# Probabilities of a neighbourhood-attention stage: five TensorE transposes per unit replaced by a split in place and one DMA transpose

## What is computed

```
s_loc = einsum('bwhd,biwjhd->bhwij', qr, kwin) * ATTN_SCALE + bias     # 8 x 16 keys around the query
s_ctx = einsum('bwhd,bchd->bhwc', qr, kc) * ATTN_SCALE                 # 256 context keys
p = softmax(concatenate([s_loc, s_ctx], axis=-1))
o = p_loc @ vwin + p_ctx @ vc
```

## Time and profile before

| what | value |
|---|---|
| median of 3 runs | 1250.49 us (1248.52 to 1252.25) |
| span of the profiled execution | 1246.6 us |
| median less the span | 3.9 us (start and end, around the span) |
| PE busy | 1226.5 us (98% of the span) |
| DVE, ACT, POOL busy | 979.6, 653.0, 398.3 us |
| the 32 units: first score to last transpose | about 268 to 380 us |

### The profile page before, as it was taken

The page is one execution under the profiler, slowest core; times in us unless marked ns, Lnnn a source line. Parts: engine busy times, 40 slices in busy tenths (PEclk is TensorE's granted clock), DMA queues, the critical chain, the costliest instruction groups (busy, mean ns, idle before and its releaser), DMA issues. The chain is left out here.

```text
span 1246.6 us, 22702 instructions
## 1 busy us (share of the span) xinstructions
PE 1226.5 (98%) x8085; PEld 668.1 (54%) x8085; DVE 979.6 (79%) x1597; ACT 653.0 (52%) x1231; POOL 398.3 (32%) x385
## 2 busy tenths in 40 slices
PE   7999999999999999999999999999999999999998
PEld 1564656556775666664454555554555554444444
DVE  3879998676778999964479888888888885666587
ACT  2642234556779999963145554455555543412425
POOL 0000000114678988850320444445554430000001
PEclk9999999999999999999999999999999999999999
DMA  9728723235210130121300332322223307997963
GB/s 354 282 87 318 260 78 136 68 87 155 67 35 2 35 136 9 29 86 51 118 34 1 102 102 84 92 85 66 87 90 101 101 28 265 336 339 249 351 228 135
DMA packets 111043, 164.35 MB, mean 132 GB/s; under 512 B 8560, under 2 KB 70000, under 8 KB 109552
## 3 DMA queue, kind: packets, MB, share of 16 engines
q1 hardware_dynamic: 110960, 163.24, 38.5%
HBM read 138.57 MB, written 22.55 MB: 129 GB/s over the span
## 5 line engine op out<-in xcount | busy, mean ns | idle before, releaser
L1327 PE MATMUL PS<-arena 128*128 128x512 f16 (+9 forms) x7485 | 1185.2, 319 | 13.1 <-DMA arena<-in_w_mod 5.7
L1327 PEld LDWEIGHTS PS<-arena 128*128 128x128 f16 (+3 forms) x7485 | 617.3, 100 | 555.3 <-issue 33.5
L3133 DVE SCALAR_TENSOR_TENSOR arena<-arena 128x512 f16<-128x512 f32 x128 | 111.6, 878 | 30.6 <-ACT arena L2361 29.8
L2361 ACT ACTIVATE arena<-arena 128x512 f16<-128x512 f32 x120 | 75.4, 631 | 103.2 <-PE PS L1327 103.2
L2491 ACT ACTIVATE arena<-arena 128x512 f16<-128x512 f32 x77 | 48.1, 629 | 124.7 <-DVE arena L3354 74.6
L3017 DVE TENSOR_REDUCE arena<-PS 128x1 f32<-128x512 f32 (+1 forms) x160 | 106.8, 680 | 3.3 <-PE PS L1327 3.3
L1321 POOL TENSOR_TENSOR arena<-arena 128x1 f32<-128x1 f32 x8 | 4.7, 598 | 231.3 <-DVE arena L3521 227.9
L2262 ACT ACTIVATE arena<-PS 128x512 f16<-128x512 f32 x125 | 75.7, 605 | 2.8 <-PE PS L1327 1.8
L1171 POOL TENSOR_TENSOR arena<-arena 128x512 f16<-128x512 f32 x64 | 74.0, 1158 | 8.0 <-ACT arena L2265 5.4
L3190 DVE TENSOR_TENSOR arena<-PS,arena 128x256 f32<-128x256 f32 (+1 forms) x100 | 55.2, 553 | 25.9 <-PE PS L1327 25.6
L3369 DVE SCALAR_TENSOR_TENSOR arena<-arena 128x512 f16<-128x512 f32 x77 | 52.2, 687 | 18.9 <-ACT arena L2491 18.8
(11 more groups left out here) (227 smaller groups left out, 1321.0 us busy)
## 6 DMA issues: line engine op xcount, KB each, us to landing
...
arena<-lay_bias SPq DMA_DIRECT2D x12, 512.0 KB, 3.9
...
```

What stands on the lines that cost most here:

```text
L1327: return pe.matmul(out, lhsT, rhs, start=start, stop=stop, skip_group_check=True)
L2361: act.activation(block_split(p, b)[:, 0], weight_block(p, b, first), ACT.Copy, scale=WS).then_inc(blk_hi, 1)
L3133: dve.scalar_tensor_tensor(dst[:, 1], src, WS, dst[:, 0], ALU.mult, ALU.subtract).then_inc(blk_lo, 1)
```

## The change

The fp32 probabilities are no longer turned by PE. ACT and DVE take the high and the low fp16 half of the unturned probabilities from SBUF (one instruction each of 640 columns, into `Phl`, three buffers), and SP issues one DMA transpose per unit that turns the 1280 fp16 columns of both halves at once from `Phl` into `PT` (three buffers). It waits for the low half, for the transpose two units earlier and for the weighing three units earlier. `weigh` moves from two slots behind to three, and behind the quarter projection of its slot; `scaled` moves from two behind to four. `scores(k)` waits for `exponentials(k-2)` and no longer for the first piece of `low_p(k-2)`. The bias pieces are issued one at a time between the transposes, the output weights in parts of 256 KB (the first MB between the transposes, the others after the last unit), and four of GpSimd's eight `scale_out` move into the groups 1 to 4 of the next stage. Several buffers move in SBUF, and `exponentials(0)` waits for what lay in the place of `Pb`.

```diff
-        self.banks = [range(0, 3), range(3, 5)]
+        self.third = v % 3
         self.scores_at = 1024 * self.par
-    def turned(self, bank):
-        return 2 * self.v + bank + 1
-    def turned_at(self, bank):
-        if bank == 1:
-            return 512 * (6 + self.par) + 256
-        return self.scores_at + 5 * P
+    def turned_in(self):
+        return 16 * (self.v // 2 + 1 + self.par)
...
-        rcp = f32(2.4375, 2)
+        rcp = f32(2.4375, 8)
...
-        Pb = [f32(o, 5, P) for o in (103, 105.5)]
-        PT = [[f16(o, 5, P) for o in parts] for parts in ((28, 29.25), (30.5, 100))]
-        nearV = [f16(o, 4, HN, 2, HD) for o in (20, 24, 32, Z + 91)]
-        bias = [f32(o, 1024) for o in (4, 8, 36, 40, 44)]
+        Pb = [f32(o, 5 * P) for o in (12, 14.5)]
+        Phl = [f16(o, 2, 5 * P) for o in (100, 102.5, 105)]
+        PT = [f16(o, 2 * 5, P) for o in (46, 48.5, 17)]
+        nearV = [f16(o, 4, HN, 2, HD) for o in (20, 24, 28, Z + 91)]
+        bias = [f32(o, 1024) for o in (4, 8, 32, 36, 40)]
...
-        q2 = [f16(48 + i, 512) for i in range(2)]
-        shifts = f16(102, GROUP * P)
+        q2 = [f16(44 + i, 512) for i in range(2)]
+        shifts = f16(51, GROUP * P)
...
-            sp.wait_ge(pr_mm, GROUP0[0])
-            for n in range(BIAS_EARLY, BIAS_EARLY + BIAS_RING):
-                load_bias(n)
-            sp.wait_ge(late_rdy, 4)
-            for n in range(2):
-                t0 = (16, 40)[n]
-                sp.dma_start(gates[n].rearrange("(t p) -> p t", p=P), mod[:, t0:t0 + 8, 0],
-                             allow_slow_non_contiguous=True).then_inc(gates_out, 16)
-            sp.wait_ge(s_max, n_scored(BiasPiece(BIAS_EARLY - 1).units_done - 1))
-            for n in range(2):
-                load(chunk_index("wo", n), w_out[:, 0:4, 512 * n:512 * n + 512], (4, 512))
-            for n in range(BIAS_EARLY + BIAS_RING, 3 * HN):
-                load_bias(n)
-            for n in range(2, 4):
-                load(chunk_index("wo", n), w_out[:, 4:8, 512 * (n % 2):512 * (n % 2) + 512], (4, 512))
+            def load_wo(n, k):
...
+                if n == RING_P - 1:
+                    pool.wait_ge(o_mm, NNA)
...
-                for i in ((), (0,), (1,), (2,), (3,), (4, 5), (6, 7), ())[u - GROUP0[0]]:
+                for i in ((), (0,), (1,), (2,), (3,), (), (), ())[u - GROUP0[0]]:
...
+                    if n == 3 and 1 <= g <= 4:
+                        scale_out(g + 3)
...
-            def copied(u, bank):
-                pe.wait_ge(pt_lo, u.turned(bank))
...
-                    copied(u.ahead(-2), 0)
+                    pe.wait_ge(s_exp, u.v - 1)
...
-            def turn_p(u):
-                pe.wait_ge(s_exp, u.v + 1)
-                for b, bank in enumerate(u.banks):
-                    if b == 1 and u.v >= 2:
-                        pe.wait_ge(o_rdy, u.v - 1)
-                    for i in bank:
-                        o = u.turned_at(b) + (i - bank.start) * P
-                        ins = pe.transpose(PSf[:, o:o + P], Pb[u.par][:, i], ident)
-                    ins.then_inc(pt_mm, 1)
             def weigh(u):
+                if u.v == 0:
+                    pe.wait_ge(near_in[0], 16 * 13)
+                if u.v == 3:
+                    pe.wait_ge(near_in[1], 16 * 5)
                 if u.v >= 2:
                     pe.wait_ge(o_rdy, u.v - 1)
-                copied(u, 1)
+                pe.wait_ge(pt_in[u.par], u.turned_in())
...
-                        ins = mm(PS[:, 6 + u.par, 0:HD], PT[u.par][part][:, i], v[:, vp],
+                        ins = mm(PS[:, 6 + u.par, 0:HD], PT[u.third][:, 5 * part + i], v[:, vp],
...
-            pe.wait_ge(pr_n, n_normed(first - 2))
-            turn_p(Unit(0))
             turn_qk(first - 2)
             project_q(first, 0)
             pe.wait_ge(pr_tc, first - 2)
             scores(Unit(1))
             project_q(first, 1)
-            pe.wait_ge(near_in[0], 16 * 13)
-            weigh(Unit(0))
             turn_qk(first - 1)
             project_q(first, 2)
             scores(Unit(2))
+            project_q(first, 3)
             pe.wait_ge(pr_vl, n_valued(first - 1))
             pe.wait_ge(pr_n, n_normed(first - 1))
-            turn_p(Unit(1))
-            project_q(first, 3)
             for k in range(3, NNA):
                 if k == 4:
                     pe.wait_ge(pr_tc, first)
-                if k == 5:
-                    pe.wait_ge(near_in[1], 16 * 5)
                 scores(Unit(k))
                 if early_chunk(k) == 0:
                     pe.wait_ge(pr_tc, first + 1)
@@ -1793,20 +1802,20 @@
                     turn_shifts(Step(0))
                 if q_unit(k, 5) is not None:
                     turn_qk(q_unit(k, 5))
-                weigh(Unit(k - 2))
-                turn_p(Unit(k - 1))
                 for i in range(4):
                     if q_unit(k, i - 3) is not None:
                         project_q(q_unit(k, i - 3), i)
+                weigh(Unit(k - 3))
                 if early_chunk(k) == NKT:
                     chunk(Step(NKT))
             step(Step(0))
+            weigh(Unit(NNA - 3))
+            step(Step(1))
             weigh(Unit(NNA - 2))
-            turn_p(Unit(NNA - 1))
-            step(Step(1))
             step(Step(2))
+            step(Step(3))
             weigh(Unit(NNA - 1))
-            for s in range(3, BODY):
+            for s in range(4, BODY):
                 step(Step(s))
...
             def exponentials(u):
+                if u.v == 0:
+                    act.wait_ge(late_used, 2 * CHUNKS.count("late"))
+                    act.wait_ge(split_lo, 9)
+                if u.v >= 2:
+                    act.wait_ge(pt_lo, u.v - 1)
                 act.wait_ge(s_max, n_scored(u.v))
-                act.activation(flat(Pb[u.par]), PSf[:, u.scores_at:u.scores_at + 5 * P], ACT.Exp,
-                               scale=-1.0, bias=nmax[:, u.par:u.par + 1], accum_out=esum[:, u.v % 4:u.v % 4 + 1])\
-                    .then_inc(s_exp, 1)
+                act.activation(Pb[u.par], PSf[:, u.scores_at:u.scores_at + 5 * P], ACT.Exp, scale=-1.0,
+                               bias=nmax[:, u.par:u.par + 1], accum_out=esum[:, u.v % 4:u.v % 4 + 1]).then_inc(s_exp, 1)
             def copy_p(u):
-                if u.v >= 2:
-                    act.wait_ge(o_mm, u.v - 1)
-                for b, t in enumerate(u.banks):
-                    act.wait_ge(pt_mm, u.turned(b))
-                    o = u.turned_at(b)
-                    act.activation(flat(PT[u.par][0][:, t.start:t.stop]), PSf[:, o:o + len(t) * P],
-                                   ACT.Copy, scale=PSC).then_inc(pt_hi, 1)
+                if u.v >= 3:
+                    before = u.ahead(-3)
+                    act.wait_ge(pt_in[before.par], before.turned_in())
+                act.wait_ge(s_exp, u.v + 1)
+                act.activation(Phl[u.third][:, 0], Pb[u.par], ACT.Copy, scale=PSC)\
+                    .then_inc(pt_hi, 1)
             def scaled(u):
                 if u.v == 0:
+                    act.wait_ge(near_in[0], 16 * 13)
                     act.wait_ge(near_in[1], 16 * 5)
                 act.wait_ge(rcp_rdy, u.v + 1)
                 act.wait_ge(o_mm, u.v + 1)
                 act.activation(natok[:, u.j, u.blk * HD:u.blk * HD + HD], PS[:, 6 + u.par, 0:HD],
-                               ACT.Copy, scale=rcp[:, u.par:u.par + 1]).then_inc(o_rdy, 1)
+                               ACT.Copy, scale=rcp[:, u.v % 8:u.v % 8 + 1]).then_inc(o_rdy, 1)
...
             exponentials(Unit(0))
             hi_parts(first - 2)
+            copy_p(Unit(0))
             from_psum(first - 1)
             turned(first - 3)
-            copy_p(Unit(0))
+            exponentials(Unit(1))
             turned(first - 2)
+            copy_p(Unit(1))
             hi_parts(first - 1)
-            exponentials(Unit(1))
             turned(first - 1)
             for k in range(2, NNA):
                 if q_unit(k, 1) is not None:
                     from_psum(q_unit(k, 1))
                 if q_unit(k, 5) is not None:
                     turned(q_unit(k, 5))
-                if k > 2:
-                    scaled(Unit(k - 2))
-                copy_p(Unit(k - 1))
                 exponentials(Unit(k))
-                if k == 2:
-                    act.wait_ge(near_in[0], 16 * 13)
-                    scaled(Unit(0))
+                if k >= 4:
+                    scaled(Unit(k - 4))
                 if q_unit(k, 3) is not None:
                     hi_parts(q_unit(k, 3))
+                copy_p(Unit(k))
                 if early_chunk(k) is None and free_bank(k)[0] is not None:
                     copy_shifts(Step(0))
+            scaled(Unit(NNA - 4))
             step(Step(0))
-            scaled(Unit(NNA - 2))
-            copy_p(Unit(NNA - 1))
+            scaled(Unit(NNA - 3))
             step(Step(1))
             step(Step(2))
+            scaled(Unit(NNA - 2))
```

(19 more changed lines are left out.)

52 lines of the change are left out of this document (44 added, 8 removed).

## The result

The changed kernel takes **1274.95 us** (1274.0 to 1280.62), the kernel before, run beside it, 1249.51 (1248.52 to 1252.25): ratio 1.021, 95% interval 1.0185 to 1.0234. It is 25.4 us slower, where 1253 had been forecast in a range up to 1259.

What follows compares the result with a forecast made beforehand. PE alone was taken as full in the touched stage, with a query-tile loop nearly as long behind it. On 1250.5 us, +3.5 - 2.4 + 0.5 + 0 + 2.0 - 1.0 = +2.6 gave 1253 us, range 1243 to 1259.

Steps and rivals of the forecast that it cites:

- SP's new waits hold back only such loads: On SP's queue: the new waits delay only loads used four units or more later; a load ahead costs at most 1.5 us.
- Loop after ... I take 12.6.: Loop through the query tiles in the neighbourhood stage: 12.6 us per period against PE's 12.58 before, so gain per period 0.
- Both copies from SBUF ... no change: ACT's high and DVE's low half read from SBUF: no more than 0.75 and 0.9 us, taken as no change.
- +3.5 us on PE: Start of the stage: ACT's new order delays PE's turn to 284.6, with PE idle some 5 us.
- the first period runs at PE's own pace: First period behind the start: 2.9 us of transposes saved less 0.47 for `weigh(0)`, so -2.4 us.
- Rival 2: Start: PE's idle 5 us drops its clock from 2.4 to 1.2 GHz, +3 us, 1256 in all; chance 0.16.
- The DMA transpose, 3.15 us: SP's transpose of 320 KB per unit lands in 3.15 us (2.4 to 8), hidden in the steady stage.
- Rival 3: Transposes land late for PE's weighing: decides from a landing of about 5.6 us; at 8 us, 1276; chance 0.10.
- Tail +2.0: End of the stage: PE waits 1.9 and 0.8 us for transposes of units 30 and 31, starving ACT: +2.0 us.
- Moved `scale_out` ... I take 0 (up to +1): Four GpSimd scalings of 1.5 us moved into the next stage's groups cost 0, up to +1 us.
- The weighing behind the projection ... 0.47: `weigh` now stands between projection and score in the query-tile loop, adding 0.47 us.
- Output weights, -1.0: Start: spreading the 2 MB of loads may free PE's 1.5 us wait on issue, -1.0 us (0 to -1.5).

Runs made afterwards that it cites:

- e1_gates: The changed kernel with the two gate copies issued behind the loads of x1, not between the transposes of units 3 and 4: 1267.77 us, ratio 1.0153.
- e2_scale: e1_gates with DVE's scaling of the query projection ahead of the maximum of the scores in every fourth unit: 1260.48 us, ratio 1.0094.
- e3_low_psum: e1_gates with DVE's low half reading its first operand from PSUM (scores times zero, value left out), the next scores waiting for it: 1260.03 us, ratio 1.0081.
- e5_start: e2_scale with ACT's order at the start of the stage as before the change, the probabilities' copies and exponentials of unit 1 later: 1256.90 us, ratio 1.0058.
- e17_before_scale: The kernel before with only GpSimd's four output-weight scalings moved beside groups 1 to 4 of the global attention: 1253.02 us beside 1249.89, ratio 1.0016.
- e4_weigh: e1_gates with PE weighing unit k-3 ahead of the query projection, not behind it: 1262.40 us, ratio 1.0107.
- e7_mix: e2_scale with unit k-3 weighed between query transposes and projection, in units where PE transposes a query unit: 1261.29 us, ratio 1.0089.
- e8_all: e7_mix plus the start order of e5_start and GpSimd's four moved output-weight scalings given to DVE: 1253.06 us, ratio 1.0024.
- e11_mix: e10_tailweigh with the weighing of unit k-3 between query transposes and projection, as in e7_mix: 1251.74 us, ratio 1.0016.
- e12_psum: e10_tailweigh with exponentials written over the scores in PSUM, where ACT and DVE read them, value kept: 1249.93 us, ratio 1.0.
- e10_tailweigh: e5_start plus four scalings on DVE, GpSimd's first output-weight scaling one query unit later, units 29 and 30 weighed one step later: 1252.70 us, ratio 1.0021.

## Why the prediction was wrong

It read the kernel before rightly: the loop through the query tiles was there, PE's freed time became waits, and the gain per period was nothing. The direction was open in the forecast (slower by over 0.3% had 0.37), the size was not: nothing in it reached 1275 but a rival with another cause.

1. **"SP's new waits hold back only such loads"** failed. The sentence counted loads behind SP's waits; the trouble was the reverse, transposes behind SP's other DMAs. The two gate copies are plain in the diff, in the same loop, and were never priced. They cost 7.2 us (e1_gates; 9.6 in the profiles): the transpose behind them landed after 13.7 us, not 3.15 and the 1.5 that the prediction allowed for a load ahead of it.
2. **"Loop after ... I take 12.6."** The links were right, two sizes were not. It is the term with the largest error beside the gates: 0 was put down for the periods, and they lost 10.9 us. "Both copies from SBUF ... no change" asked what they cost ACT and DVE (0.73 and 0.82 us, as said), not what DVE's second operand in SBUF does to GpSimd: from its first rotation to ACT's high half 5.11 us for 4.16. And the 2.53 us from projection to maximum were taken at the full clock; they were 3.99 where the clock fell and 2.49 where it did not. So a period is 14.9 us with both and 13.4 with the stretch alone, for the 12.6 taken. The six periods behind the stop lose 2.7, 2.3, 2.2, 0.9, 1.5 and 1.3 us; the first of them holds GpSimd's wait for the output weights, which was not in the sum either. e2_scale takes 7.3 us out by shortening the loop, e3_low_psum 7.7 by taking GpSimd's stretch out of it and with it the slow clock.
3. **The start, "+3.5 us on PE"** was right in its mechanism and size: PE's turn starts 2.4 us later (283.50 for 281.14), 3.3 counted from the first maximum of the stage, and PE idles 4.5 us. With e5_start the first period's copy comes 4.2 us sooner and the kernel is 3.6 us faster. What failed is the -2.4 behind it, "the first period runs at PE's own pace": it began at 1.2 GHz. At full clock it is oversized too: in e5_start PE waits 1.7 us there for 0.2 before, and the first copy is level with before, so some 1.4 us are won and not 2.4. Rival 2 (clock at the start, 0.16) was true, at about 1.4 us for its 3, but the prediction let the clock fall only there. It fell again after two of the pairs of pauses in mid stage, and not after others of nearly the same length; why, no run shows.
4. **The DMA transpose, 3.15 us:** measured 3.3 to 3.4 in undisturbed use, inside its bounds, and hidden in most units (PE waited 5.6 us in 6 waits in e1_gates). Rival 3's arithmetic (from a landing of 5.6 us it decides) was not tested by a slow transpose; the one late landing came from the queue. Its two prices block by block did not come about, the 6.0 us from an issue of 0.6 us per block and the estimate of 13.1 us from the 1309 ns that the Trainium skill has for one 128x128 block by DMA (VectorE: DVE Perf Modes, The three transpose paths). One instruction of 1.35 us moves all ten blocks and lands in 3.4 us; the price of a single block no run here shows.
5. **"Tail +2.0":** PE did wait for the last transposes, 1.34, 0.24 and 1.19 us for units 29, 30 and 31, where the prediction has 0, 1.9 and 0.8; the last period of the stage is 13.05 us for 11.75, +1.3. The size is near, the places are not.
6. **"Moved `scale_out` ... I take 0 (up to +1)"** failed: 2.3 us in the trace of after, 2.0 to 3.1 alone in e17_before_scale. The prediction's own figures left no room: 9.0 us and 1.5 are 10.5 in a group of 10.3. And what room a busy share of 14.82 in 17 shows is not where the operation stands: some 1.3 us of each of the two scalings shown reached the end of their group.
7. **"The weighing behind the projection ... 0.47":** its sign holds on the long loop, but its size is not shown: of the 5.4 us in e4_weigh 3.5 lie in the two periods whose clock no longer falls. On the short loop it was worth nothing (e7_mix).
8. **Output weights, -1.0:** no run of its own. PE's wait of 1.5 us at 294 is not in the trace of after, but nothing shows that the loads made it: in e17_before_scale the same wait is for DVE's low half. What the runs do show has the other sign: GpSimd waited 4.65 us for the first part (2.8 in e1_gates), and moving the scaling that waits was worth 1.5 us of a period (13.98 in e8_all, 12.48 in e11_mix).

By the medians, 25.4 us are 7.2 for the gates, 7.3 for the period as far as DVE's order heals it, 3.6 for the start and 2 to 3 for the scalings; of the remaining 4 to 5, taking GpSimd's stretch out gave 2.8 (e12_psum over e10_tailweigh), and the rest is smaller than what these runs resolve. These parts were measured one on top of another, so another order would share them out otherwise.

Open: what holds e12_psum's period at 12.36 us. PE waits there 8.8 us for DVE's low halves and 6.6 for ACT's turned copies in the whole stage, and no run took both away. Open too: why the clock fell after some pairs of pauses and not after others, and whether the gates are slow for their 4-byte elements or for something else, since no run kept them in their place in another shape.
